# First expert block fed from resident x by a selection product, final root table loaded early, last output tile in two halves

## The reference

```python
h = modulate(rms_norm(x, norm_ffn_g[l]), sh_f, sc_f).reshape(-1, d)
# hier_moe: each token takes the best of 4 groups, and in it the best 2 of 8 experts
gates = jnp.sum(jax.nn.one_hot(eid, MOE_EXPERTS) * w[..., None], axis=1)
for e in range(MOE_EXPERTS):                       # 32 experts
    hid = jax.nn.silu(h @ w1[e]) * (h @ w3[e])     # 1024 -> 512
    out = out + gates[:, e:e + 1] * (hid @ w2[e])  # 512 -> 1024
x = x + g_f * f.reshape(x.shape)
return rms_norm(x, final_norm_g)
```

## Time and profile before

| | |
|---|---|
| runs of the kernel before | 995.97, 998.24, 993.85 us |
| median | 995.97 us |
| profiled execution | 995.65 us |
| its span, first to last instruction | 993.9 us |
| PE busy in the span | 885.2 us (89%) |
| DVE, ACT, POOL busy | 420.5, 244.6, 139.2 us |
| bytes moved | 263.58 MB |
| mean granted clock of TensorE | 0.963 |

### The profile page before, as it was taken

The page is one execution under the profiler, slowest core; times in us unless marked ns, Lnnn a source line. Parts: engine busy times, 40 slices in busy tenths (PEclk is TensorE's granted clock), DMA queues, the critical chain, the costliest instruction groups (busy, mean ns, idle before and its releaser), DMA issues.

```text
span 993.9 us, 12760 instructions
## 1 busy us (share of the span) xinstructions
PE 885.2 (89%) x4459; PEld 442.1 (44%) x4459; DVE 420.5 (42%) x1072; ACT 244.6 (25%) x558; POOL 139.2 (14%) x374
## 2 busy tenths in 40 slices
PE   4699999999989989999889999999999986767885
PEld 1455546644445555546534444444444433332332
DVE  3586888643488646035812223122221321211124
ACT  4511023102267664114011111111111211111112
POOL 1401001020000000001011122122121321221210
PEclk9799999999999999999899999999999998989998
DMA  9952203456710220134869999999999999999946
GB/s 339 349 181 46 85 0 113 110 172 240 268 41 1 106 106 2 30 139 171 337 262 389 397 421 416 418 420 420 421 420 420 419 418 418 419 418 419 419 180 260
DMA packets 52629, 263.58 MB, mean 265 GB/s; under 512 B 11187, under 2 KB 13547, under 8 KB 25712
## 3 DMA queue, kind: packets, MB, share of 16 engines
q1 hardware_dynamic: 40320, 246.04, 61.5%
q0 software_dynamic: 12096, 17.00, 6.3%
q10 hardware_dynamic: 176, 0.05, 0.0%
HBM read 265.66 MB, written 22.01 MB: 289 GB/s over the span
## 4 chain that ended last, share of the span: by engine, by line
PE 46%; issue 23%; SPq 13%; DMA 8%; DVE 5%; POOL 3%; ACT 2%; POOLq 1%; DVEq 0%; ACTq 0%
PE PS L757 14%; SPq L384 10%; PE PS L1013 6%; PE PS L939 4%; DMA S5Z<-in_moe_w 3%; DMA BIG<-in_w_mod 3%; PE PS L946 2%; PE PS L699 2%; PE PS L976 2%; PE PS L644 2%; DMA BIG<-xh_d,gidx 2%; PE PS L1099 2%; SPq L389 1%; POOL held L583 1%; PE PS L985 1%
## 5 line engine op out<-in xcount | busy, mean ns | idle before, releaser
L757 PE MATMUL PS<-BIG 128*128 128x512 f32 (+2 forms) x352 | 139.9, 553 | 0.0
L757 PEld LDWEIGHTS PS<-BIG 128*128 128x128 f32 x352 | 64.1, 190 | 68.2 <-issue 67.8
L1199 PE MATMUL PS<-BIG,GM 128*64 128x512 f32 x336 | 79.5, 616 | 5.7 <-DMA BIG<-in_moe_w 4.6
L1180 PE MATMUL PS<-S5Z,QKV 128*128 128x512 f32 x192 | 83.4, 592 | 0.0
L1177 PE MATMUL PS<-BIG,QKV 128*64 128x512 f32 x288 | 65.9, 609 | 7.3 <-DMA BIG<-in_moe_w 5.5
L583 POOL TENSOR_TENSOR held<-held 1x1 f32<-1x1 f32 x147 | 27.3, 185 | 312.0 <-PE PS L1153 172.3
L2332 DVE TENSOR_TENSOR QKV<-PS,QKV 64x512 f32<-64x512 f32 x50 | 34.4, 688 | 79.1 <-PE PS L1199 46.9
L1513 ACT ACTIVATE QKV<-PS,fcp 128x128 f32<-128x128 f32 x128 | 48.3, 458 | 58.5 <-PE PS L1153 58.5
L1170 PE MATMUL PS<-BIG,QKV 128*32 128x256 f32 x768 | 48.1, 402 | 13.8 <-DMA BIG<-in_moe_w 13.8
L1013 PE MATMUL PS<-BIG 128*128 128x512 f32 x128 | 56.1, 595 | 0.0
L2312 DVE TENSOR_SCALAR QKV<-PS,fcp 128x128 f32<-128x128 f32 x128 | 43.7, 404 | 28.0 <-PE PS L1153 28.0
(11 more groups left out here) (493 smaller groups left out, 1179.2 us busy)
## 6 DMA issues: line engine op xcount, KB each, us to landing
BIG<-in_moe_w SPq DMA_DIRECT2D x84, 1024.0 KB, 20.7
BIG<-in_moe_w SPq DMA_DIRECT2D x21, 2048.0 KB, 23.7
S5Z<-in_moe_w SPq DMA_DIRECT2D x40, 1024.0 KB, 19.0
BIG<-in_w_mod SPq DMA_DIRECT2D x12, 2048.0 KB, 7.9
S5Z<-in_moe_w SPq DMA_DIRECT2D x10, 2048.0 KB, 22.6
...
```

The costliest lines, as they stand in the source:

```text
L757: ins = mm(dst[:, c0:width], hT[:, k, tok], wslot(n, width)[:, k, c0:width], start=(k == 0), stop=(k == KD - 1))
L1180: ins = mm(bank(2 + m), hgT[:, k, :], w13(side)[:, m, k, :], start=(k == 0), stop=(k == KD - 1))
L1199: ins = mm(PS[64 * n:64 * n + 64, 2560:3072], hidT[:, k % 2, 64 * (k // 2):64 * (k // 2) + 64], w2s(side)[:, k, 512 * n:512 * (n + 1)], st ...
```

## The change

Four things change.

1. **Block 0's rows come from `XN`.** DVE builds, for each of the four tiles of tokens, a 128 x 64 matrix `own` that holds the reciprocal root of the token's row where the token stands in that lane of block 0, and zero elsewhere. PE multiplies it with x: eight products, of 64 columns of `own` against 512 words of x, two column groups side by side in PS. The words of x are taken in an order that puts the four k-groups of one half together, `(q k)[:, :, 4n:4n+4]`: runs of four words, eight words apart. ACT copies the result to `sg`, PE turns it by eight transposes of 64 rows, ACT alone applies the modulation into `hgT0`, and `up(0)` uses it. All that, with `up(0)`, stands ahead of PE's wait for `routed`.
2. **The gather for block 0 is gone.** POOL's first gather is block 1's, at the place where block 0's was. SP's w2 of side 2 no longer waits for gathered rows.
3. **The gates' five steps on DVE** move from behind `slots` to ahead of the wait for `filled`.
4. **Last stage.** ACT loads the root's table right behind its last block, and the silu table before `routed`. Tile 3 is scaled and stored in two halves of 512 columns.

```diff
@@ -213,6 +213,9 @@
         ysb = QKV[:, 6144:7168]
         hid = GM[:, 0:512]
         hidT = GM[:, 512:1024].rearrange("p (k s) -> p k s", k=4)
+        own = GM[:, 0:256].rearrange("p (t l) -> p t l", t=NLT)
+        lanes_at = GM[:, 256:320]
+        hgT0 = GM[:, 512:1024].rearrange("p (k s) -> p k s", k=KD)
         sg = wglu[:, :, :].rearrange("p k n -> p (k n)")
         rt = S5Z[:, 8192:11520]
...
@@ -418,7 +421,6 @@
                 load13(0, 2, 0, piece)
             sp.wait_ge(sem("slots"), 2)
             sp.wait_ge(sem("routed"), 1)
-            sp.wait_ge(sem("hg_in"), 16)
             load2(0, 2)
             last = sp.value_load(btab[0:1, NBLK + 2:NBLK + 3], min_val=0, max_val=NTRI) + 3
...
             for t in range(NLT):
-                sp.wait_ge(sem("fin"), t + 1)
-                sp.dma_start(out[0, t * P:(t + 1) * P, :], XN[:, t, :]).then_inc(sem("out_done"), 16)
-            sp.wait_ge(sem("out_done"), 16 * NLT)
+                for c in (slice(0, D // 2), slice(D // 2, D)) if t == NLT - 1 else (slice(0, D),):
+                    sp.wait_ge(sem("fin"), t + 1 + c.start // (D // 2))
+                    sp.dma_start(out[0, t * P:(t + 1) * P, c], XN[:, t, c]).then_inc(sem("out_done"), 16)
+            sp.wait_ge(sem("out_done"), 16 * (NLT + 1))
...
-            pool.tensor_copy(gidx[:, :], slots[:, 0:1, 0]).then_inc(sem("gidx"), 1)
+            pool.tensor_copy(gidx[:, :], slots[:, 1:2, 0]).then_inc(sem("gidx"), 1)
             pool.wait_ge(sem("gidx"), 1)
             pool.indirect_dma_start(hg, None, xh_d, bass.IndirectOffsetOnAxis(gidx[:, 0:1], 0),
...
@@ -602,8 +605,6 @@
                 pool.indirect_dma_start(pair_d, bass.IndirectOffsetOnAxis(sidx[:, 0:1], 0), ysb, None,
                                         bounds_check=TOPK * LAT, oob_is_err=False).then_inc(sem("y_sc"), 16)
 
-            hold(sem("hg_tr"), 1)
-            gather(1)
             hold(sem("hg_tr"), 2)
             gather(2)
...
@@ -1125,7 +1126,14 @@
             mm(bank(6, NE, 192), qb_b[0:NE, :], opp128[0:NE, :], start=True, stop=False)
             mm(bank(6, NE, 192), hb_b[0:NE, :], tri128[0:NE, :], start=False, stop=True)
             mm(bank(6, NE, 224), hb_b[0:NE, :], ident[0:NE, 0:NE], start=True, stop=True).then_inc(sem("place"), 1)
-            warm(8)
+            warm(10)
+            pe.wait_ge(sem("own"), 1)
+            for t in range(NLT):
+                for n in range(2):
+                    ins = mm(PS[64 * n:64 * n + 64, 1024:1536].rearrange("p (q k) -> p q k", k=KH), own[:, t, :],
+                             XN[:, t, :].rearrange("p (q k) -> p q k", k=KD)[:, :, KH * n:KH * (n + 1)],
+                             start=(t == 0), stop=(t == NLT - 1))
+            ins.then_inc(sem("made"), 1)
             for k in range(TOPK):
                 pe.wait_ge(sem("spread"), k + 1)
...
@@ -1136,19 +1144,11 @@
             mm(PS[0:1, 3584:3584 + NBLK], ones[0:NE, 0:1], cmph[0:NE, :], start=True, stop=False)
             mm(PS[0:1, 3584:3584 + NBLK], wexp[0:NE, :], cmpq[0:NE, :], start=False, stop=False)
             mm(PS[0:1, 3584:3584 + NBLK], wexp[0:NE, :], cmpf[0:NE, :], start=False, stop=True).then_inc(sem("bt"), 1)
-            warm(3)
-
-            pe.wait_ge(sem("routed"), 1)
-
-            mixed = pe.value_load(btab[0:1, NBLK:NBLK + 1], min_val=0, max_val=NTRI) + 1
-            small = pe.value_load(btab[0:1, NBLK + 1:NBLK + 2], min_val=0, max_val=NTRI) + 2
-            last = pe.value_load(btab[0:1, NBLK + 2:NBLK + 3], min_val=0, max_val=NTRI) + 3
 
             def turn_rows(b):
-                pe.wait_ge(sem("hg_in"), 16 * b + 16)
-                if not isinstance(b, int) or b >= 1:
-                    pe.wait_ge(sem("hgT_a"), b)
-                    pe.wait_ge(sem("hgT_d"), b)
+                pe.wait_ge(sem("hg_in"), 16 * b)
+                pe.wait_ge(sem("hgT_a"), b)
+                pe.wait_ge(sem("hgT_d"), b)
                 for k in range(KD):
                     ins = tr(bank(k // 4, P, (k % 4) * P), hg.rearrange("p (q k) -> p k q", k=KD)[:, k, :], ident)
...
                                 r = slice(64 * m, 64 * m + 64)
-                                ins = mm(PS[r, 1024:1536].rearrange("p (m h) -> p m h", m=2), hgT[:, k, 64:128],
+                                ins = mm(PS[r, 1024:1536].rearrange("p (m h) -> p m h", m=2), few,
                                          w13(side)[:, :, k, 256 * m:256 * m + 256], start=(k == 0), stop=(k == KD - 1))
                             else:
                                 ins = mm(bank(2 + m), hgT[:, k, :], w13(side)[:, m, k, :], start=(k == 0), stop=(k == KD - 1))
                     ins.then_inc(sem("w13_used"), 1)
+
+            pe.wait_ge(sem("own_out"), 1)
+            for n in range(2):
+                r = slice(64 * n, 64 * n + 64)
+                for k in range(KH):
+                    ins = tr(bank(n, 64, k * P), sg[r, k * P:(k + 1) * P], ident[r, r])
+                ins.then_inc(sem("made" if n == 0 else "hg_tr"), 1)
+            up(0, "half", 0, 1)
+            pe.wait_ge(sem("routed"), 1)
+
+            mixed = pe.value_load(btab[0:1, NBLK:NBLK + 1], min_val=0, max_val=NTRI) + 1
+            small = pe.value_load(btab[0:1, NBLK + 1:NBLK + 2], min_val=0, max_val=NTRI) + 2
+            last = pe.value_load(btab[0:1, NBLK + 2:NBLK + 3], min_val=0, max_val=NTRI) + 3
 
             def turn_hid(b, size):
                 pe.wait_ge(sem("hid"), b + 1)
@@ -1213,10 +1227,6 @@
                 down(b - 1, size_before, j, i)
                 turn_hid(b, size)
 
-            warm(3)
-            turn_rows(0)
-            warm(2)
-            up(0, "half", 0, 1)
             turn_rows(1)
             turn_hid(0, "half")
...
@@ -1232,7 +1242,7 @@
             down(3 * last, "half", 0, last + 1)
 
             warm(12, 7)
-            pe.wait_ge(sem("gates"), 1)
+            pe.wait_ge(sem("diag"), DH + 1)
             for t in sum_of:
...
@@ -1500,8 +1510,18 @@
                   bank(4, P).rearrange("p (h b c a) -> p b h a c", h=2, b=2, a=8)[:, b], ACT.Copy).then_inc(sem("e_exp"), 1)
 
 
+            act.wait_ge(sem("perm_in"), 16)
+            act.wait_ge(sem("made"), 1)
+            A(sg.rearrange("p (k q) -> p k q", k=KH), bank(2).rearrange("p (q k) -> p k q", k=KH), ACT.Copy).then_inc(
+                sem("own_out"), 1)
+            for piece, (signal, count, done) in enumerate((("made", 2, "hgT_a"), ("hg_tr", 1, "hgT_d"))):
+                act.wait_ge(sem(signal), count)
+                for k in range(KH * piece, KH * (piece + 1)):
+                    ins = A(hgT0[:, k, :], bank(piece, 64, (k % 4) * P), ACT.Identity, scale=fcp[:, 0, k:k + 1], bias=fcp[:, 1, k:k + 1])
+                ins.then_inc(sem(done), 1)
+            A(silu_t[:, 0:1], epsb[:, :], ACT.Silu)
+
             act.wait_ge(sem("routed"), 1)
-            act.wait_ge(sem("perm_in"), 16)
 
             mixed = act.value_load(btab[0:1, NBLK:NBLK + 1], min_val=0, max_val=NTRI) + 1
...
@@ -1542,7 +1562,6 @@
 
 
             act.wait_ge(sem("slots"), 2)
-            rows_T(0)
             step(0, "half")
             with act.Fori(1, mixed + 1) as i:
...
@@ -1554,8 +1573,9 @@
                 for j in range(3):
                     step(3 * i - 2 + j, "half")
 
+            A(silu_t[:, 0:1], epsb[:, :], ACT.Sqrt)
             for t in range(NLT):
-                act.wait_ge(sem("summed" if t in sum_of else "x_out"), t // 2 + 1)
+                act.wait_ge(sem("made" if t in sum_of else "x_out"), t // 2 + (3 if t in sum_of else 1))
                 root_ms(sum_of[t] if t in sum_of else XN[:, t, :], D, sml[:, 40 + t:41 + t], "f_ms", junk2)
 
...
@@ -2213,6 +2233,10 @@
             for i in range(2):
                 st(ts(virt[:, i:i + 1], n_all, -1.0 - i, None, ALU.add))
             st.settle()
+            dve.wait_ge(sem("e_exp"), 3)
+            st(ts(left, virt[:, 0:1], float(P), None, ALU.mult))
+            st.settle()
+            st(ts(lanes_at, lanes[:, 0:64], left, None, ALU.add))
             dve.wait_ge(sem("place"), 1)
 
...
             st.settle()
+            st(tt(wts[:, 7, :], pos[:, 0], pos[:, 1], ALU.max))
+            st.settle()
+            for t in range(NLT):
+                ins = ts(own[:, t, :], lanes_at, wts[:, 7, t:t + 1], sml[:, 36 + t:37 + t], ALU.is_equal, ALU.mult)
+                if t < NLT - 1:
+                    st(ins)
+            ins.then_inc(sem("own"), 1)
             st(ts(blk, pos, -(P - 1) / 2.0, 1.0 / P, ALU.add, ALU.mult))
             st.settle()
             st(ts(blk, blk, MAGIC, MAGIC, ALU.add, ALU.subtract))
             st.settle()
...
@@ -2256,6 +2286,16 @@
             st.settle()
             ts(cmph[0:NE], virt[0:NE, :], endv[0:NE, 2:3], None, ALU.is_ge).then_inc(sem("cmp"), 1)
 
+            dve.wait_ge(sem("g_exp"), 1)
+            dve.wait_ge(sem("e_exp"), 1)
...
@@ -2268,17 +2308,6 @@
             st(stt(row, empty, none[:, 1:2], got[:, 1, :], ALU.mult, ALU.add))
             st.settle()
```

(16 more changed lines are left out.)

17 lines of the change are left out of this document (12 added, 5 removed).

## The result

The changed kernel takes 993.49 us (median of 22 runs), the kernel before 996.99 us (22 runs beside it, one of them a slow one of 1066.73 us that the ratio leaves out). The medians differ by 3.5 us; the ratio is 0.9961, 95% interval 0.9950 to 0.9972, which is 3.9 us less. Forecast were 6.7 us less. The profiled execution took 993.34 us with a span of 991.6 (before: 995.65 and 993.9).

A forecast was written before the change was run, and what follows sets the result against it. The experts' weight stream at a fixed 420 GB/s was taken as the bound, so its start counts. Stream 5.2 plus last stage 1.5 gave 6.7 us: 995.65 to 989.0 us, 80% range 986.5 to 994.3.

The forecast's parts named there:

- the path to `up(0)`: Block 0's start: `up(0)` begins at about 500.1 us instead of 506.10, 6.0 us earlier.
- the pace of the products: Picked rows' eight products on PE read x in runs of four at the adjacent-word pace: 3.55 us.
- the w2: Start of the weight stream: SP issues this transfer at 499.6 us instead of 501.32.
- the idle 2.26 us: PE's idle time ahead of L1132 before the change; claimed to be gone after it.
- the stream, 5.2 us: Experts' weight transfers start earlier without the pause at 508 to 512; last byte lands 5.2 us earlier, bounds 4.0 and 6.0.
- The rival on the clock at `up(0)`: PE's clock falls at `up(0)`: 991.6 us, chance 0.12 of full price; if partly slow, cost under 1 us.
- the last stage, 1.5 us: Kernel's end: earlier root table 0.95, halves' extra cost -0.1, smaller last store 0.6; 1.5 us less, bounds 0.8 and 2.0.
- All behind it on DVE follows: Last stage: finish 1 begins 0.95 us earlier, and the last finish starts at about 988.6 instead of 989.54.
- the halves: Last tile: two-part scaling costs about 0.1 us more, storing 256 KB instead of 512 KB last saves 0.6 us.
- PE doesn't wait for `own`: Ahead of the picked rows' products: ten warm products at 0.68 us each end at 490.8, `own` is posted at about 490.3.
- Slow reading of runs of four: Rival at the picked rows' products: slower x reads use up the gain at f = 2.9; chance 0.05 above, 0.07 near 2.
- the stream's whole gain given back: Rival: a later wait in the weight stream eats the earlier start, only the last stage's 1.5 us stay: 994.1; chance 0.14.

The follow-up runs named there:

- warm_sum: Changed kernel with two warm products between tile 0's sum and the wait for tile 2's results: 992.3 us, ratio 0.9951.
- whole_tile: Changed kernel with its last tile scaled and stored in one piece again: 992.6 us, ratio 0.9949.
- again_2: Changed kernel, unaltered, measured once more on another run's chip: 991.79 us, ratio 0.9942.
- before_2: Kernel before, unchanged, for a second trace: 998.43 us.
- late: Changed kernel with fifteen warm products instead of ten ahead of the picked rows' products, and three ahead of `up(0)`: 997.03 us, ratio 1.001.
- no_wait: Kernel before without SP's wait for block 0's rows ahead of block 2's w2: 998.01 us, ratio 1.0007.
- before_3: Kernel before, unchanged, for a third trace: 998.49 us.
- tail_only: Kernel before with the last stage's edits alone (root table early, last tile in halves): 995.76 us, ratio 0.998.
- few_fill: Changed kernel with seven warm products instead of ten ahead of `own`, plus fills before `up(0)` and the last sums: 989.3 us, 0.9928; repeated: 988.27 us, 0.9926.

## Why the prediction was off

**Right: the path to `up(0)` and the pace of the products.** 6.1 us earlier against 6.0, 3.65 us against 3.55, the w2 1.75 us earlier against 1.7; the idle 2.26 us went.

**Right where the clock is up in the routing: the stream, 5.2 us.** From the mask product to the last stage: before 491.7, changed 487.7 and 486.8, hence 4.1 and 4.9 us, under the forecast but inside its bounds of 4.0 and 6.0. warm_sum and whole_tile, the same program up to the last stage, took 485.6 and 485.1, so single traces scatter here by 2.6 us. The rival on the clock at `up(0)` came true in its mild form ("the w2's 5 us of transfer cover most"): up to 2.9 us longer on PE, and no loss behind that can be seen.

**Failed: the last stage, 1.5 us.** Measured: 0.4 us longer in two of three traces of the changed kernel, 1.3 us less in the third. The step that failed is "All behind it on DVE follows". It follows only as long as the last rows land early and PE's sum of tile 2 is quick.

*The rows' landing.* In the old stage DVE waits for the root's table load anyway. In the new one it goes straight from tile 1's sum to the first scaling, so its wait for tile 1's rows is on the path. In again_2 they let DVE start 7.69 us behind SP's load, in the changed kernel's first trace 8.12, in others up to 8.78. before_2 and late have them late, by 8.49 and 8.47, and the sum of tile 2 quick in both:

```profile
982.15 1.28 DVE L2370 SCALAR_TENSOR_TENSOR QKV<-BIG,wts,QKV 128x1024 f32<-128x1024 f32 x1 [11.41 <-DMA BIG<-pair_d]
...
985.20 0.17 DVE L2360 RECIPROCAL sml<-sml 128x1 f32<-128x1 f32 x1 [0.45 <-ACT sml L1280]
```

```profile
976.96 1.28 DVE L2400 SCALAR_TENSOR_TENSOR QKV<-BIG,wts,QKV 128x1024 f32<-128x1024 f32 x1 [11.67 <-DMA BIG<-pair_d]
...
979.48 0.15 DVE L2389 RECIPROCAL sml<-sml 128x1 f32<-128x1 f32 x1
```

The old stage takes 23.0 us all the same, for DVE still waits for ACT; the new one takes 22.4 instead of 21.7. What sets the landing stays open; rows that let DVE start only after 8.0 us or more came in 2 of the 5 traces with the old first block and in 8 of the 13 with the new one.

*The sum's clock.* PE waits 1.4 to 2.6 us for tile 2's rows, and in four of the nine traces that have this wait and the early root, the products behind it ran at the lower clock (5.40 us for 3.70). In the three traces of before and in no_wait, after 1.4 to 2.25 us of waiting, they never did. That doesn't prove that the edit brings the fall: all four falls came behind waits of 1.87 us or more, where the kernels with the old root have two traces without a fall, and late has another; behind waits of 1.5 us and less there is none in six traces, old root or early. What the rows do show is that a slow sum costs more now. In before_3 ACT has the root of tile 2 1.5 us before DVE takes its reciprocal, in tail_only 0.4 us:

```profile
988.73 0.29 ACT L1280 ACTIVATE sml<-sml,epsb 128x1 f32<-128x1 f32 x1
...
990.54 0.16 DVE L2360 RECIPROCAL sml<-sml 128x1 f32<-128x1 f32 x1
```

```profile
989.83 0.29 ACT L1281 ACTIVATE sml<-sml,epsb 128x1 f32<-128x1 f32 x1
...
990.50 0.15 DVE L2362 RECIPROCAL sml<-sml 128x1 f32<-128x1 f32 x1
```

By that the old stage would hide 1.5 us of the 1.7; I have no run of it. In the changed kernel's first trace DVE waits 1.27 us for that root, and starts tile 1's sum 0.4 us late: together most of the 1.8 us between its 23.5 and the 21.7 of again_2. I weighed the clock at `up(0)`, where no cost shows, and not here, where the sum is on the path. Even with early rows and full clock the term is 1.3 to 1.4: the halves give 0.3 us, not 0.6 - 0.1 = 0.5.

**Failed: one trace taken for all.** "PE runs ten warm products ... from 483.96 to 490.8. So PE doesn't wait for `own`" holds but for 0.27 us where the clock is up: 6.72 us. (`own` was 0.6 us later than dated; DVE's last four steps for it alone took 0.98 us, where the prediction had 1.0 for seven.) Where it is down they take 8.53, the products ahead are late as well, and the w2 goes out at 24.87 behind the mask product, where the kernel before issues it at 22.76: 2.1 us later, not 1.7 earlier. From the mask product to the last stage that gives 490.8 (again_2) against 493.1 and 493.7 (before_3, before_2), 2.6 us instead of 4 to 5. The filler was priced at 0.68 us a product from a row at full clock, and I didn't ask what it costs at half. Of the 4.4 us by which own is late there, 3.0 are the filler's (again_2), the rest comes from the small products ahead.

**The sum.** From the mask product to the end of the span, before took 514.8, 516.7 and 516.3 us, changed 511.1, 510.2 and 512.5: in the mean 515.9 and 511.3, or 4.6 us, beside 3.9, 4.9 and 5.8 us by the three ratios. Of the 6.7 us forecast, up to 1.9 are missing in the last stage in such executions as have late rows and a slow sum, and some 2.6 at the start of the stream where the routing's clock is down. How often each happens among the timed runs no trace tells, so that the shares of the two in the 2.8 us can't be settled. That they are most of it is what the version that works on both suggests: few_fill's two traces take 509.1 and 506.3 us from the mask product, its ratios give 7.2 and 7.4 us. It also holds the three products ahead of `up(0)`, which showed no gain, and late rows it can't mend (22.4 us of last stage in its first trace). No single edit of it is clear of the noise by itself.

**Ruled out.** Slow reading of runs of four (3.65 us), and the stream's whole gain given back (late, and the 4.1 and 4.9 us above).
